# The second down projection with tokens on the partitions, added onto the transposed residual in PSUM

## The reference

```python
def rms_norm(x, gain):
    y = x * lax.rsqrt(jnp.mean(x * x, axis=-1, keepdims=True) + NORM_EPS)
    return y * gain

def conv_ffn(h, w_up, conv_w, conv_b, w_down):          # D_FF = 2816
    a, gate = jnp.split(h @ w_up, 2, axis=-1)
    a = causal_depthwise_conv(a, conv_w) + conv_b
    return (jax.nn.silu(a) * gate) @ w_down

# per layer
x = x + attention(rms_norm(x, attn_norm[i]))
x = x + conv_ffn(rms_norm(x, ffn_norm[i]), ...)
# after both layers
return rms_norm(x, final_norm)                          # [1, 512, 1024]
```

## Time and profile before

| | |
|---|---|
| three runs, us | 1219.69, 1221.59, 1222.01 |
| median, us | 1221.59 |
| span of the profiled execution, us | 1220.8 |
| TensorE busy | 1172.3 us, 96% |
| VectorE, ScalarE, GpSimd busy | 60%, 39%, 38% |
| TensorE clock granted, mean | 0.988 of full |
| DMA | 101.44 MB, mean 83 GB/s |
| out<-x_tok, 8 DMAs | 256.0 KB each |

### The profile page before, as it was taken

One profiled execution on the slowest core, in us unless ns is written; L12 is line 12 of the kernel. 1 busy time (PEld: TensorE's weight loads), 2 busy tenths in 40 slices (PEclk: granted clock), 3 DMA queues, 4 the chain that ended last, 5 costly groups with the idle time before them and its releaser, 6 DMA issues.

```text
span 1220.8 us, 16338 instructions
## 1 busy us (share of the span) xinstructions
PE 1172.3 (96%) x5820; PEld 988.4 (81%) x5820; DVE 726.4 (60%) x948; ACT 473.4 (39%) x929; POOL 464.0 (38%) x240
## 2 busy tenths in 40 slices
PE   7999899999999999999999999889999999999997
PEld 6988777888888878887988888768888888878885
DVE  5577766677777761115567666755777777751114
ACT  6556645322222222324554555643322222222325
POOL 4211307344443435445332222324444344425441
PEclk8999999999999999999999999999999999999998
DMA  7211103333333312324322311105333333222322
GB/s 217 67 35 35 61 10 104 104 103 86 86 103 103 86 52 86 103 87 137 104 53 59 86 46 34 40 30 137 82 91 103 103 103 85 71 68 86 103 95 78
DMA packets 146476, 101.44 MB, mean 83 GB/s; under 512 B 12065, under 2 KB 139270, under 8 KB 146438
## 3 DMA queue, kind: packets, MB, share of 16 engines
q1 hardware_dynamic: 146438, 100.93, 28.3%
HBM read 98.82 MB, written 2.10 MB: 83 GB/s over the span
## 4 chain that ended last, share of the span: by engine, by line
issue 73%; POOL 23%; ACT 1%; POOLq 1%; DMA 1%; DVE 1%; PE 0%; SPq 0%; DVEq 0%
POOL w_lo L486 23%; DMA raw<-in_a_w_in 1%; POOLq L490 0%; POOLq L485 0%; ACT w_hi L964 0%; ACT y_feat L982 0%; ACT sq L987 0%; DVE ssacc L1283 0%; DVE x_tok L1625 0%; DVE xT L1505 0%; ACT h_hi L982 0%; SPq L369 0%; PE ps L537 0%; PE ps L499 0%; PE ps L501 0%
## 5 line engine op out<-in xcount | busy, mean ns | idle before, releaser
L486 POOL TENSOR_TENSOR w_lo<-raw,w_hi 128x512 fp32r<-128x512 f32 (+2 forms) x212 | 461.0, 2190 | 733.9 <-ACT w_hi L964 733.9
L499 PE MATMUL ps<-h_hi,w_lo 128*128 128x512 f32 x704 | 274.7, 390 | 0.0
L501 PE MATMUL ps<-h_hi,w_hi 128*128 128x512 f32 x704 | 273.9, 389 | 0.0
L500 PE MATMUL ps<-h_lo,w_hi 128*128 128x512 f32 x704 | 273.9, 389 | 0.0
L964 ACT ACTIVATE w_hi<-raw 128x512 fp32r<-128x512 f32 (+2 forms) x212 | 192.7, 941 | 139.8 <-PE ps L501 139.6
L1531 DVE SCALAR_TENSOR_TENSOR conv<-normed,vecT,conv 128x510 f32<-128x510 f32 x44 | 189.3, 4303 | 5.9 <-DVE conv L1529 1.5
L499 PEld LDWEIGHTS ps<-h_hi,w_lo 128*128 128x128 f32 x704 | 132.2, 188 | 28.0 <-issue 0.5
L500 PEld LDWEIGHTS ps<-h_lo,w_hi 128*128 128x128 f32 x704 | 132.2, 188 | 27.7 <-issue 0.5
L501 PEld LDWEIGHTS ps<-h_hi,w_hi 128*128 128x128 f32 x704 | 132.2, 188 | 27.4
L499 PE MATMUL ps<-u_hi,w_lo 128*128 128x512 f32 x352 | 138.8, 394 | 4.8 <-DVE u_all L1536 4.5
L1518 DVE TENSOR_TENSOR u_lo<-u_all,u_hi 128x512 fp32r<-128x512 f32 x44 | 30.4, 692 | 187.8 <-ACT u_hi L1151 187.8
(11 more groups left out here) (169 smaller groups left out, 1621.3 us busy)
## 6 DMA issues: line engine op xcount, KB each, us to landing
raw<-in_ffn_w_up SPq DMA_DIRECT2D x88, 512.0 KB, 5.0
raw<-in_ffn_w_down SPq DMA_DIRECT2D x44, 512.0 KB, 3.3
raw<-in_b_w_in SPq DMA_DIRECT2D x24, 512.0 KB, 5.1
raw<-in_a_w_out SPq DMA_DIRECT2D x4, 1024.0 KB, 5.0
raw<-in_b_w_out SPq DMA_DIRECT2D x4, 1024.0 KB, 5.0
raw<-in_a_w_in SPq DMA_DIRECT2D x3, 1024.0 KB, 7.1
x_tok<-in_x SPq DMA_DIRECT2D x4, 512.0 KB, 4.8
out<-x_tok SPq DMA_DIRECT2D x8, 256.0 KB, 2.9
```

What stands on the lines that cost most here:

```text
L486: pool.tensor_tensor(w_lo[:, s, at], raw[:, s, at], w_hi[:, s, at].bitcast(F32), ALU.subtract).then_inc(lo_done, 1)
L499: pe.matmul(out_, a_lo, b_hi, start=start, stop=False)
L500: pe.matmul(out_, a_hi, b_lo, start=False, stop=False)
L501: return pe.matmul(out_, a_hi, b_hi, start=False, stop=stop)
```

## The change

In layer 1 only, the down projection is turned round. A piece of `u` (128 tokens) is held and the weights stream: a token tile t has two banks, 2t and 2t+1, each 128 tokens by 512 features. Still 24 matmuls of 128x512 a block. The residual is not added by DVE: before the first matmul of a token tile, PE transposes the 8 pieces of `xT` into its two banks (`seed`), and the matmuls add onto them. The token tiles 2 and 3 are seeded at once behind the up phase, 0 and 1 where their banks come free. The last pair is interleaved so that the token tiles finish one after the other.

The final norm then works per token tile, straight from PSUM: ACT squares both banks and sums along the row, DVE makes the bias out of the first sum, ACT does Ln and Exp, DVE multiplies each bank by the reciprocal root and the gain and writes `x_tok`, SP stores each half as it comes. The gain is no longer a column per feature chunk (`vrow`, `vecT`) but a row copied to all partitions, loaded by one DMA into `htmp` in the up phase of layer 1. `y_feat`, `back`, the adds, the squares' sum and `mean_square_tok` for the end are gone.

```diff
@@ sync @@
-            sp.dma_start(vrow[R_FINAL:R_FINAL + KC, 1, :],
-                         final_norm.rearrange("(f p) -> f p", p=P)).then_inc(vec_landed, 16)
...
+                if ph == "up1":
+                    sp.wait_ge(olo_done, NT * UA + UB)
+                    sp.dma_start(gain_end.rearrange("p a b -> p (a b)"), final_norm.partition_broadcast(P))\
+                      .then_inc(gain_end_landed, 16)
...
-                sp.wait_ge(y_dve if b % 2 else y_act, b // 2 + 1)
-                at = slice(b // NT * half, (b // NT + 1) * half)
-                sp.dma_start(ov[:, b % NT, at], x_tok[:, b % NT, at]).then_inc(stored, 16)
+                sp.wait_ge(y_out, b + 1)
+                at = slice(b % 2 * half, (b % 2 + 1) * half)
+                sp.dma_start(ov[:, b // 2, at], x_tok[:, b // 2, at]).then_inc(stored, 16)
@@ tensor @@
+            def seed(t):
+
+                for h in range(2):
+                    for c in range(4):
+                        pe.matmul(ps[:, 2 * t + h, c * P:(c + 1) * P], xT[:, 4 * h + c, t * P:(t + 1) * P],
+                                  ident[:, :], is_transpose=True, start=(c == 0), stop=False)
+
+            def down_tok_pair(r, is_first, is_last):
+
+                ph = "down1"
+                if is_first:
+                    order = [(0, 2), (0, 3), (0, 0), (0, 1)] + [(1, t) for t in range(NT)]
+                elif is_last:
+                    order = [(0, 0), (0, 1), (1, 0), (0, 2), (1, 1), (0, 3), (1, 2), (1, 3)]
+                else:
+                    order = [(s, t) for s in range(2) for t in range(NT)]
+                if is_first:
+                    seed(2)
+                    seed(3)
+                begun = set()
+                for s, t in order:
+                    if s not in begun:
+                        pe.wait_ge(lo_done, part_done(ph, r * 2 + s))
+                        pe.wait_ge(ulo_done, r * 2 + (FB + s + 1))
+                        begun.add(s)
+                    if is_first and s == 0 and t < 2:
+                        pe.wait_ge(u_done, 2 * FB - 1 + t)
+                        seed(t)
+                    tok = slice(t * P, (t + 1) * P)
+                    for h in range(2):
+                        c = slice(h * T, (h + 1) * T)
+                        ins = hi_lo(ps[:, 2 * t + h, :], u_hi[:, s, tok], u_lo[:, s, tok],
+                                    w_hi[:, s, c], w_lo[:, s, c], start=False, stop=(is_last and s == 1))
+                        if is_last and s == 1:
+                            ins.then_inc(down_done, 1)
+                    if not (is_last and s == 1) and (s, t) == [x for x in order if x[0] == s][-1]:
+                        ins.then_inc(down_used, 1)
...
-            def back(dc, tiles):
...
-            mean_square_tok(NORM["end"])
@@ scalar @@
+                if l == 1:
+                    act.preload_act_table_set("natural_log_exp_and_others")
                 with act.Fori(0, FB // 2 - 1) as r:
...
-                        gained(NORM["end"], dc, vecT[:, 1, R_FINAL + dc:R_FINAL + dc + 1])
-                        square(NORM["end"], dc)
...
+            for t in range(NT):
+                for h in range(2):
+                    act.wait_ge(down_done, KC + 2 * t + h + 1)
+                    act.activation(sq[:, h, :], ps[:, 2 * t + h, :], ACT.Square,
+                                   accum_out=y_ss[:, t, h:h + 1]).then_inc(y_sq, 1)
+                act.wait_ge(y_sq, 2 * t + 2)
+                act.wait_ge(y_based, t + 1)
+                act.activation(y_rstd[:, t:t + 1], y_ss[:, t, 1:2], ACT.Ln, bias=y_bias[:, t:t + 1],
+                               scale=1.0 / D).then_inc(y_ln, 1)
+                act.wait_ge(y_ln, t + 1)
+                act.activation(y_rstd[:, t:t + 1], y_rstd[:, t:t + 1], ACT.Exp, scale=-0.5).then_inc(y_root, 1)
@@ vector @@
-                    add_to_stream(NORM["end"], down_done, KC, range(KC), None)
...
+            def base(t):
+
+                dve.wait_ge(y_sq, 2 * t + 1)
+                dve.tensor_scalar(y_bias[:, t:t + 1], y_ss[:, t, 0:1], 1.0 / D, EPS, ALU.mult, ALU.add)\
+                   .then_inc(y_based, 1)
+
+            dve.wait_ge(gain_end_landed, 16)
+            base(0)
+            for t in range(NT):
+                dve.wait_ge(y_root, t + 1)
+                for h in range(2):
+                    dve.scalar_tensor_tensor(out=x_tok[:, t, h * T:(h + 1) * T], in0=ps[:, 2 * t + h, :],
+                                             scalar=y_rstd[:, t:t + 1], in1=gain_end[:, h, :], op0=ALU.mult,
+                                             op1=ALU.mult).then_inc(y_out, 1)
+                if t + 1 < NT:
+                    base(t + 1)
```

More of the change, by code:

```diff
@@ L137, in trunk @@
         gainB = sb("gainB", [P, 1])
+        y_ss = sb("y_ss", [P, NT, 2])
+        y_bias = sb("y_bias", [P, NT])
+        y_rstd = sb("y_rstd", [P, NT])
         cos16 = sb("cos16", [P, NT, ROT])
@@ L922, in _ @@
             feed_forward(1)
-            def back(dc, tiles):
-                for t in tiles:
-                    at = slice(dc % 4 * P, (dc % 4 + 1) * P)
-                    ins = pe.transpose(ps[:, dc // 4 * NT + t, at],
-                                       y_feat[:, dc, t * P:(t + 1) * P], ident[:, :])
-                    if dc % 4 == 3:
-                        ins.then_inc(y_tr, 1)
-            pe.wait_ge(x_ready, KC * NORM["end"] + 4)
-            for dc in range(4):
-                pe.wait_ge(y_done, dc + 1)
-                back(dc, range(NT))
-            pe.wait_ge(x_ready, KC * NORM["end"] + 7)
-            for dc in range(4, 7):
-                pe.wait_ge(y_done, dc + 1)
-                back(dc, range(3))
-            pe.wait_ge(y_done, KC)
-            back(7, range(3))
-            mean_square_tok(NORM["end"])
-            pe.wait_ge(ln_done, NORM["end"] + 1)
-            for dc in range(4, KC):
-                back(dc, (3,))
         @block.scalar
@@ L980, in gained @@
                 act.wait_ge(x_ready, KC * norm + dc + 1)
-                dst, done = (y_feat, y_done) if norm == NORM["end"] else (h_hi, hhi_done)
-                act.activation(dst[:, dc, :], xT[:, dc, :], ACT.Copy, scale=gain).then_inc(done, 1)
+                act.activation(h_hi[:, dc, :], xT[:, dc, :], ACT.Copy, scale=gain).then_inc(hhi_done, 1)
             def square(norm, dc):
@@ L1263, in _ @@
             feed_forward(1)
-            act.wait_ge(rstd_done, NORM["end"] + 1)
-            for b in range(0, 2 * NT, 2):
-                act.wait_ge(y_tr, b + 1)
-                act.activation(x_tok[:, b % NT, b // NT * (D // 2):(b // NT + 1) * (D // 2)], ps[:, b, :],
-                               ACT.Copy, scale=rstd_tok[:, b % NT:b % NT + 1]).then_inc(y_act, 1)
+            for t in range(NT):
[9 more added lines that the diff above has]
+                act.activation(y_rstd[:, t:t + 1], y_rstd[:, t:t + 1], ACT.Exp, scale=-0.5).then_inc(y_root, 1)
         @block.vector
```

61 lines of the change are left out of this document (31 added, 30 removed).

## The result

Twenty runs of each kernel: median 1222.52 us after (1220.75 to 1224.11) and 1220.95 us before (1218.09 to 1223.75). The ratio is 1.0013, interval 1.0007 to 1.0019. The changed kernel is 1.6 us slower on the medians, less than 0.2%, where it was forecast to be 7.0 us faster: 8.6 us are missing. Yet the profile shows nearly every step that was forecast.

What follows compares the result with a forecast made beforehand. PE was taken to bound the down phase, with the tail behind it open to attack. Gains of 0.3 (first pair) and 8.0 (tail) less 1.3 (stall) took 1221.59 to 1214.6 us; range 1212.7 to 1217.0.

Steps and rivals of the forecast that it cites:

- The loop: Layer 1's down matmuls with u held and weights streaming: no cost taken, ends 0 and 5.3 us over 528 matmuls.
- The clue that the step went by: Projection with h held: 38 matmuls of 384 columns in 6.30 us, 0.43 ns a column against 0.44 in the down phase.
- The first pair: Start of layer 1's down phase: transposes fill PE's wait for `u_all`, no slow clock, 0.3 us gained.
- The last pair: End of layer 1's down phase: PE waits about 1.6 us for both parts of `w_lo`; last matmul 1.0 us later.
- The tail: From the last down matmul to the span's end: 14.5 us become 6.4.
- The sum: Whole kernel: +0.3 first pair, -1.3 stall, +8.0 tail, 7.0 us faster.
- The clock fell neither in the stall: Rival: the clock falls in the last pair's stall or over the seeds, costing 1.7 us, to 1216.3; chance 0.13.
- The stores don't queue: Rival at the end: stores queue and squares take longer, 1.7 us more, 1216.3; chance 0.10.
- Slower: the exchanged roles make each down matmul longer: Rival in layer 1's down phase: pitch 0.240 breaks even, 0.246 gives 1224.9; chance 0.03 shared with the serialised tiles.
- The token tiles weren't serialised: Rival at the end: ACT or DVE serialise the tiles until the last matmul, last store 1224.4; chance 0.03 shared with longer matmuls.
- I am wrong if the pitch moves: Sign in the profile after: the down matmuls' pitch should stay at 0.226, else the forecast is wrong.

Runs made afterwards that it cites:

- experiment 5: Changed kernel with its three small end tiles laid in free attention tiles plus padding, so large tiles lie where they were before: 1213.55 us, ratio 0.9941.
- experiments 2 and 3: Kernel before with 32 unused bytes, behind `rden` (1230.09 us, ratio 1.0065) or ahead of `u_hi` alone (1226.69 us, ratio 1.0044).
- experiment 9: Kernel before with 64 bytes of padding ahead of the weights, moving `w`, `ot` and `u` but not `h`: 1235.05 us, ratio 1.0115.
- experiment 4: Kernel before with `w_hi` and `w_lo` moved 32 bytes and a second pad of 32 bytes behind them: 1242.16 us, ratio 1.0174.
- experiment 6: Kernel before with 64 bytes of padding ahead of `ot` and `u`: 1223.54 us, ratio 1.0023.

## Why the prediction was wrong

It was wrong in one step, "The loop", where it says of the exchanged roles "So I take no cost". That the roles cost nothing is right (experiment 5). But the step asked only what the instructions are, and not where their operands lie. The change shifts `u` against `w` by 32 bytes, and the pitch goes from 0.2267 to 0.2333, in 1056 matmuls and not in the 528 that the step looked at. The term stood at 0 and is about 7 us (1056 x 0.0066; 6.4 between the traces of after and experiment 5), and the output projections, which no term looked at, add 1.1. The upper end kept for the term, 5.3 us, counted one layer, and the range did not take it in.

The clue that the step went by was misread as well. A window of 6.30 us with 38 matmuls also counts the one that reaches into it; by the starts the projection's pitch is 0.1740, or 0.453 ns a column, against 0.443 in the down phase. It looked no dearer and is 2% dearer by the column. Neither reading could show the shift: in the kernel before, h and w have a distance of 0.

The other terms, read in experiment 5, where the pitch is that of before:

- **The first pair.** Forecast: no wait at `u_all`, no slow clock, 0.3 us gained. The matmul that starts 28th stood 10.22 us behind the first one before; here the nineteenth starts 7.55 us behind the first seed, and nine more at 0.2267 make 9.59. The gain is 0.6: transposes and switches together were a little cheaper than 3.7 + 0.3. The gain is counted against a trace in which the clock fell. Behind the same hole it stayed up in six of twelve traces, where the phase is 1.6 us shorter; there the seeds lose about 1.0. The forecast took the slow stretch as certain, from one trace.
- **The last pair.** Forecast: a stall of about 1.6 and the last matmul 1.0 us later, counted from the up phase's end. Measured: block 21 starts 1.54 us late (1.39 of it idle), and from the first down instruction (seed or matmul) to PE's end it is 125.15 us and not 124.43, 0.7 later. With the 0.6 gained above, that is 1.3 us for the last pair, as in the forecast's sum.
- **The tail.** 6.4 forecast, 6.0 measured (5.9 after). Squares from PSUM with a row sum start 0.57 to 0.70 apart (0.66 taken) and Ln waits for `y_bias` as forecast. Two multiplications together take 1.41 us (1.50 taken), twice on this path, and the stores land in 2.0 us where I took 2.3. These two sizes are nearly the whole difference.
- **The sum** in experiment 5: 8.5 from the tail less 0.7 at PE's end is 7.8, measured 7.0 on the medians, with an interval of 5.2 to 9.2. That the medians agree with the forecast's 7.0 to the decimal is in part luck: the gain at the first pair was too small for an execution in which the clock falls there, and is a loss in one in which it doesn't.

The rivals:

1. The clock fell neither in the stall (1.00 in the row from 1203.80) nor over the seeds (1.00 from 1085.90). The Trainium skill (TensorE: Matmul & The Clock Gate, Part 4: PE-mode transpose) says that transposes don't count as PE being busy in the same way. By that, sixteen of them in a row, 1.9 us, should have done what an idle hole does in this place. The traces don't bear that out: the clock fell here in none of the five with seeds, and in six of the twelve with a hole of 2.10 to 2.25 us.
2. The stores don't queue: eight issues from 1209.4 to 1217.8, each landed 2.0 us after its issue.
3. "Slower: the exchanged roles make each down matmul longer" is nearest to what happened and still another thing. It named the resource, a longer pitch, and set its break-even at 0.240. The pitch stayed below that, at 0.2333, but in twice as many matmuls, and by an effect that is there without the roles (experiments 2 and 3). Its argument, that `u` is freshly written, is not the cause: in experiment 5 the same fresh `u` is held, and in experiment 9 it is streamed, and the pitch is 0.2267.
4. The token tiles weren't serialised; tile 0's squares began at 1206.65, 7.7 us ahead of PE's end.

The check that would have caught it was in the list ("I am wrong if the pitch moves"), but the cause could have been read from the diff: a tile's size and three new tiles ahead of `u` in the order of declaration.

What stays open: why the distance matters. The runs show which distances cost and how much; they don't show what in reading two operands collides, nor why +64 costs a third of the others. The weight loads themselves show 0.19 us at every distance. What decides whether the clock falls behind a hole of 2.2 us stays open too.

## What to carry to other kernels

When a change adds, drops or resizes any tile, print the start of every large tile before and after, and compare the operands of each hot matmul modulo 256 bytes; a pitch that changed in code nobody touched is the sign of a shift. Keep both operands of a matmul at the same remainder, and lay small new tiles into dead ones or fill up to it; that is shown here for fp32r matmuls of 128x512 with a weight load each. When PE must wait for an operand, work that it has to do anyway, such as transposes, costs little there and kept the clock up in all five traces. And don't take the clock from one trace: a slow stretch that is there in one execution may be absent in the next.

## What the runs showed of the hardware that I had not expected

- The pitch of 128x512 matmuls with a weight load for each goes from 0.2267 to 0.2289, 0.2333 or 0.2343 us, up to 3.4%, by the distance of the two operands in SBUF modulo 256 bytes alone, whether the other engines are busy or idle beside them. PE shows as 100% busy with a granted clock of 1.00 in all of them. Up phases of 2112 and down phases of 1056 such matmuls make that up to 20.9 us of 1221 (experiment 4).
- The projections of 384 columns, with the roles of h and w exchanged, hardly feel it (22.5 us for 22.3 at a distance of +32). A short matmul is a poor guide to what a longer one costs.
- The hole of 2.10 to 2.25 us in front of layer 1's down phase brought the granted clock down to 0.50 for 3.4 us in six of twelve traces and left it at 1.00 in the other six, the same instructions in front of it. Sixteen transposes of 1.9 us in the same place brought it down in none of five. Shorter holes did it at times as well, such as the 1.86 us at 64.7 in the trace of experiment 6, with 0.50 from 67.1 on. The time goes with it: of the eleven runs of the kernel before beside experiment 9, the fastest took 1217.88 us at a mean granted clock of 0.996 and the slowest 1223.46 at 0.988.
